# Cross-attention's keys and values made in the modulation stage and kept in DRAM

## The reference

```
x = x + memory_cross_attention(rms_norm(x, norm_xattn[l]), rms_norm(mem, norm_mem[l]), wq[l], wkv[l], wo[l])

q = (xn @ wq)                    # 4 heads of 128
kv = (memn @ wkv)                # keys and values, 4 heads each: 1024 columns
p = softmax(q k^T / sqrt(128))
o = (p v) @ wo
```

## Time and profile before

| | us |
|---|---|
| median of 3 runs | 3963.09 (3961.88 to 3965.83) |
| the profiled execution | 3962.45 |
| its span | 3961.1 |
| TensorE busy | 3767.7 (95%) |
| VectorE busy | 2579.8 (65%) |
| ScalarE busy | 1794.8 (45%) |
| POOL busy | 1484.2 (37%) |

### The profile page before, as it was taken

The page is one execution under the profiler, slowest core; times in us unless marked ns, Lnnn a source line. Parts: engine busy times, 40 slices in busy tenths (PEclk is TensorE's granted clock), DMA queues, the critical chain, the costliest instruction groups (busy, mean ns, idle before and its releaser), DMA issues.

```text
span 3961.1 us, 64430 instructions
## 1 busy us (share of the span) xinstructions
PE 3767.7 (95%) x27348; PEld 3208.4 (81%) x27348; DVE 2579.8 (65%) x3660; ACT 1794.8 (45%) x2792; POOL 1484.2 (37%) x726
## 2 busy tenths in 40 slices
PE   6898999999999999989999999999889999999998
PEld 3787888787877887888788888888778878888887
DVE  0436644785378897669879667876657775445457
ACT  1446443654355444445444444444545553333334
POOL 0332443133323440004354444444644434444443
PEclk8999999999999999999999999999899999999999
DMA  9653765355534552015366465657345435554553
GB/s 389 250 233 133 285 242 208 147 208 194 218 149 170 183 186 91 23 73 185 140 198 233 183 237 195 225 223 275 147 159 204 171 128 192 190 191 174 191 190 128
DMA packets 60848, 746.92 MB, mean 189 GB/s; under 512 B 7040, under 2 KB 9216, under 8 KB 17168
## 3 DMA queue, kind: packets, MB, share of 16 engines
q1 hardware_dynamic: 49536, 696.74, 46.5%
q0 software_dynamic: 8960, 43.95, 2.9%
q10 hardware_dynamic: 2064, 2.10, 0.2%
HBM read 725.92 MB, written 16.84 MB: 188 GB/s over the span
## 4 chain that ended last, share of the span: by engine, by line
PE 80%; DVE 12%; ACT 5%; DMA 2%; issue 1%; POOL 0%; another core or an unknown queue 0%; SPq 0%; DVEq 0%; ACTq 0%; POOLq 0%
PE ps L380 45%; PE ps L381 23%; DVE pieces L333 2%; PE ps L2283 2%; PE ps L811 2%; ACT pieces L317 2%; DMA ring<-in_ada 2%; PE ps L3652 1%; DVE opa L587 1%; DVE r L1224 1%; PE ps L1953 1%; DVE scr L608 1%; PE ps L660 1%; ACT scr L691 1%; DVE scr L392 0%
## 5 line engine op out<-in xcount | busy, mean ns | idle before, releaser
L380 PE MATMUL ps<-opa,pieces 128*128 128x512 f32 x6192 | 2241.5, 405 | 49.2 <-DVE pieces L333 32.7
L351 POOL TENSOR_TENSOR pieces<-ring,pieces 128x1024 fp32r<-128x1024 f32 x539 | 1344.8, 2495 | 2142.3 <-ACT pieces L317 2125.0
L381 PE MATMUL ps<-opa,pieces 128*128 128x256 f32 x6192 | 1739.0, 281 | 0.0
L317 ACT ACTIVATE pieces<-ring 128x1024 fp32r<-128x1024 f32 (+1 forms) x1110 | 1098.5, 1036 | 815.0 <-PE ps L381 812.8
L380 PEld LDWEIGHTS ps<-opa,pieces 128*128 128x128 f32 x6192 | 1168.6, 189 | 345.8 <-issue 33.9
L381 PEld LDWEIGHTS ps<-opa,pieces 128*128 128x128 f32 x6192 | 1174.8, 190 | 7.5 <-issue 5.0
L333 DVE TENSOR_TENSOR pieces<-ring,pieces 128x1024 fp32r<-128x1024 f32 (+1 forms) x571 | 715.4, 1253 | 257.9 <-ACT pieces L317 254.9
L380 PE MATMUL ps<-opb,pieces 128*128 128x512 f32 x2304 | 817.6, 396 | 14.1 <-DVE pieces L333 14.1
L381 PE MATMUL ps<-opb,pieces 128*128 128x256 f32 x2304 | 652.6, 283 | 0.0
L380 PEld LDWEIGHTS ps<-opb,pieces 128*128 128x128 f32 x2304 | 434.2, 188 | 123.6 <-issue 20.1
L381 PEld LDWEIGHTS ps<-opb,pieces 128*128 128x128 f32 x2304 | 434.7, 189 | 0.1
(11 more groups left out here) (450 smaller groups left out, 3568.3 us busy)
## 6 DMA issues: line engine op xcount, KB each, us to landing
ring<-in_up SPq DMA_DIRECT2D x64, 2048.0 KB, 7.7
ring<-in_down SPq DMA_DIRECT2D x64, 2048.0 KB, 7.7
ring<-in_win SPq DMA_DIRECT2D x56, 2048.0 KB, 7.8
ring<-in_ada SPq DMA_DIRECT2D x48, 2048.0 KB, 12.1
ring<-in_wout SPq DMA_DIRECT2D x24, 2048.0 KB, 8.3
ring<-in_evin SPq DMA_DIRECT2D x18, 2048.0 KB, 8.0
ring<-in_evout SPq DMA_DIRECT2D x8, 2048.0 KB, 8.1
ring<-in_xkv SPq DMA_DIRECT2D x8, 2048.0 KB, 7.8
```

The costliest lines, as they stand in the source:

```text
L317: a.do.activation(K.parts_of(p)[0][:, s, :], w[:, s, :], ACT.Copy).then_inc(*K.hi.up((p, h)))
L351: g.do.tensor_tensor(lo[:, s, :], w[:, s, :], hi[:, s, :].bitcast(F), ALU.subtract).then_inc(*K.lo2.up(p))
L380: pe.do.matmul(r3(b[:, 0:512], 2), hi[:, k, :], both(op, k), start=i == 0, stop=False)
L381: t = pe.do.matmul(b[:, 0:256], lo[:, k, :], half(op, 0, k), start=False, stop=i == kt - 1)
```

## The change

- `plan` puts the eight key/value slabs of both layers (four each, 16 tiles) at the front, in the order: key/value slab, two modulation slabs, next key/value slab. They are gone from the layers.
- The front becomes `pe_memory`, `act_memory`, `dve_memory` and `pool_memory`: tile, modulation slab, tile, modulation slab (the last two slabs after tile 14). The memory is loaded first, into the half of `x1` that will later hold the tokens, and is scaled and split into `opa` for layer 0 and `opb` for layer 1. The memory's sum of squares is taken once, in tiles 0 and 1. The context's follows in tiles 6 to 9, and `pe_norm` with its helpers goes.
- Context, tokens, constants and pooling weights load later: the context ahead of slab 3 on SyncE's queue, the rest on POOL's queue from gate tile 2 on.
- Keys and values of a layer are normalized into `xa`, the values turned, and POOL stores them to a DRAM tensor `xmem`. `pool_mem` loads 1 MB of it back ahead of cross-attention, in place of the memory.
- In `pe_xattn` the head steps (`pe_xheads`) are a side generator of the query tiles, one step after every three blocks: during tile n the values of head n-2 and scores and turnings of head n-1. Head 3 comes after the last query tile. The heads' result goes to a buffer of its own, `xop`.
- S5's column steps move from the key/value tiles to the output projection of layer 0 (its tiles 4 and on), where the memory's squares were. Two loads for S5 wait until after the last output tile of cross-attention.

```
 def plan(self):
...
-        for c in range(16):
-            raw(("ada", 0, c), ada[c])
+        for l in range(2):
+            gemm(("xkv", l), [D["xkv"][l * 4 + i] for i in range(4)])
+        tiles, todo = todo, []
+        for i in range(0, 16, 2):
+            todo.append(tiles[i])
+            for c in (i, i + 1):
+                raw(("ada", 0, c), ada[c])
+            todo.append(tiles[i + 1])
...
 def sp_weights(K):
+        if i == 3:
+            sp.do.dma_start(K.X[:, :, 256:512], r3(K.D["xin"], 16)[:, :, 256:512]).then_inc(*K.load["xctx"].up("xctx", 16))
...
 def sp_start(K):
     K.sp.do.dma_start(K.cols, K.D["cols"]).then_inc(*K.load["cols"].up("cols", 16))
+    K.sp.do.dma_start(K.X[:, :, 0:256], r3(K.D["mem"], 16)).then_inc(*K.load["mem"].up("mem", 16))
...
+def pe_memory(K):
+    pe = K.pe
+    for t in range(16):
+        l, n = divmod(t, 8)
+        side = pe_beside_memory(K, t)
+        pe_tile(K, t, K.opb if l else K.opa, ("nmem", l, "h"), (K.dve, ("xkv", l, n)), side, 5)
+        drain(side)
+        if t == 0:
+            pe.wait_ge(*K.dve.of(("silu", 1)))
+        for c in beside_memory(t):
+            pe_ada(K, 0, c, K.xb)
+            pe_turning(K)
+            K.turning = (0, c)
...
+def act_memory(K):
+    a.wait_ge(*K.load["mem"].of("mem"))
+    for k in range(16):
+        act_scaled(K, K.opa, ("nmem", 0, "h"), k, memory_block(K, k), gain(0, k))
+    act_feed(K, 0)
+    for t in range(16):
+        act_feed(K, t + 1)
+        if t < 2:
+            for k in range(8 * t, 8 * t + 8):
+                act_square(K, ("nmem",), k, memory_block(K, k), 1)
+        if t == 2:
+            act_std(K, ("nmem",), 1e-5, K.rmem)
+        if 2 <= t < 6:
+            for k in range(4 * t - 8, 4 * t - 4):
+                act_scaled(K, K.opb, ("nmem", 1, "h"), k, memory_block(K, k), gain(1, k))
...
+def dve_memory(K):
+    for k in range(16):
+        dve_scaled(K, K.opa, ("nmem", 0, "h"), k, memory_block(K, k), gain(0, k))
+    dve_feed(K, 0)
+    for t in range(16):
+        dve_feed(K, t + 1)
+        if t < 2:
+            for k in range(8 * t, 8 * t + 8):
+                dve_square(K, ("nmem",), k, 1)
+        if t == 2:
+            dve_rstd(K, ("nmem",), K.rmem)
+            v.wait_ge(*K.dve.of(("nmem", "rstd")))
+            dve_memory_out(K, 0)
+            dve_memory_out(K, 1)
...
+        if t >= 2:
+            dve_memory_out(K, t)
...
 def pool_mem(K, l):
     g.wait_ge(*K.dve.of(("mx", l, 15)))
-    g.do.dma_start(K.mem, r3(K.D["mem"], 16)).then_inc(*K.load["mem"].up(("mem", l), 16))
+    g.wait_ge(*K.load["xk_out"].of(("xk", l)))
+    g.wait_ge(*K.load["xv_out"].of(("xv", l)))
+    g.do.dma_start(K.xa, K.D["xmem"][l]).then_inc(*K.load["kv"].up(("kv", l), 16))
...
 def pe_xattn(K, l):
+    for n in range(7):
+        side = pe_xheads(K, l, h, n) if n else pe_totals(K, ("nx", l))
+        if n < 4:
+            pe_tile(K, p + n, K.opb, ("nx", l, "h"), (K.dve, ("xq", l, n)), side, 3 if n else 6)
+        drain(side)
     p = K.first["xo", l]
     for n in range(16):
-        pe_tile(K, p + n, K.opb, ("xo", l), (K.dve, ("xx", l, n)))
+        pe_tile(K, p + n, K.xop, ("xo", l), (K.dve, ("xx", l, n)))
+
+def pe_xheads(K, l, h, i):
+    if 0 <= i - 2 < 4:
+        n = i - 2
+        pe_values(K, h, n, [[K.VX[:, j, n * P:(n + 1) * P] for j in range(2)]], (K.dve, ("xo", l, n)))
+        yield
+    if 0 <= i - 1 < 4:
+        n = i - 1
+        pe.wait_ge(*K.load["kv"].of(("kv", l)))
+        pe.wait_ge(*K.dve.of(("xqn", l, n)))
+        for qt in range(2):
...
+            pe.do.matmul(b[:, 0:256], K.QX[:, n, qt * P:qt * P + P], K.KX[:, n, :], start=True, stop=True).then_inc(*K.prod.up(h.key("sc", n, qt)))
+            yield
+        for qt in range(2):
+            pe_turn(K, h, n, qt)
+            yield
```

More of the change, by code:

```diff
@@ new lines, in pe_beside_memory @@
+def pe_beside_memory(K, t):
+    if t == 2:
+        yield
+        K.pe.wait_ge(*K.load["io"].of("io"))
+        pe_total(K, ("nmem",), 1)
+        yield
+    if t == 11:
+        pe_total(K, ("n1", 0, 1))
+        yield
+    if t == 15:
+        pe_turning(K)
+        yield
+    l, n = divmod(t - 1, 8)
+    if t and n > 3:
+        yield from pe_xvturn(K, l, n - 4)
+def act_memory(K):
+    a = K.a
+    gain = lambda l, k: K.col(f"norm_mem{l}", k)
+    a.wait_ge(*K.load["mem"].of("mem"))
[12 more added lines that the diff above has]
+                act_scaled(K, K.opb, ("nmem", 1, "h"), k, memory_block(K, k), gain(1, k))
+        if t == 6:
+            a.wait_ge(*K.load["xctx"].of("xctx"))
+        if 6 <= t < 10:
+            for k in range(4 * t - 24, 4 * t - 20):
+                act_square(K, ("n1", 0, 1), k, x_at(K, 1)(k))
+        if t == 11:
+            act_std(K, ("n1", 0, 1), 1e-6, K.rstd)
+        l, n = divmod(t - 1, 8)
+        if t and n > 3:
+            act_xvturn(K, l, n - 4)
+        for c in beside_memory(t):
+            act_row(K, 0, c)
@@ L1000, in pe_gates @@
     for n in range(16):
-        pe_tile(K, p + n, K.opa, hk, (K.dve, ("gsum", l, s, n)))
+        side = pe_xvturn(K, 1, 3) if (l, s) == (0, 1) and n == 0 else None
+        pe_tile(K, p + n, K.opa, hk, (K.dve, ("gsum", l, s, n)), side)
         pe_fill(K, p + n)
@@ L1580, in pool_block1 @@
     g = K.g
+    pool_memory(K)
     pool_start(K)
@@ L2873, in act_mixout @@
         act_part(K, K.opa, ("mx", l), k, mixed(K, l, k))
+    columns = iter(()) if l else act_s5_columns(K)
     for n in range(17):
@@ L2878, in act_mixout @@
             act_ahead(K, ("nx", l), n - 1, xb(K, n - 1), ("mixo", l, n - 1), nx(n - 1), K.opb)
-        if 6 <= n < 14:
-            a.wait_ge(*K.load["mem"].of(("mem", l)))
-            for k in (2 * n - 12, 2 * n - 11):
-                act_square(K, ("nmem", l), k, K.mem[:, k, :], 1)
+        if n >= 4:
+            next(columns, None)
 def dve_mixout(K, l):
@@ L2889, in dve_mixout @@
         dve_part(K, K.opa, ("mx", l), k, mixed(K, l, k))
+    columns = iter(()) if l else dve_s5_columns(K)
     for n in range(16):
@@ L2915, in pe_xattn @@
 def pe_xattn(K, l):
-    pe, p, h = K.pe, K.first["xq", l], heads3(K, l)
-    for n in range(4):
-        side = None if n else pe_totals(K, ("nx", l), ("nmem", l))
-        pe_tile(K, p + n, K.opb, ("nx", l, "h"), (K.dve, ("xq", l, n)), side, 6)
-    p = K.first["xkv", l]
-    for n in range(8):
-        if l == 0 and n == 6:
-            pe_s5_rows(K)
-        side = pe_xvturn(K, l, n - 5) if n > 4 else None
-        pe_tile(K, p + n, K.opa, ("nmem", l, "h"), (K.dve, ("xkv", l, n)), side, 5)
-        if n > 4:
-            drain(side)
@@ L2928, in pe_xattn @@
-    drain(pe_xvturn(K, l, 3))
-    pe.wait_ge(*K.act.of(("xv", l, 3)))
-    pe.wait_ge(*K.dve.of(("xkvn", l, 7)))
-    for i in range(6):
-        if i < 4:
-            for qt in range(2):
-                b, was = K.xb.take(K.act, h.key("ex", i, qt))
-                K.bank[h.key("sc", i, qt)] = b
-                pe.wait_ge(*was)
-                pe.do.matmul(b[:, 0:256], K.QX[:, i, qt * P:qt * P + P], K.KX[:, i, :], start=True, stop=True).then_inc(*K.prod.up(h.key("sc", i, qt)))
-        if 0 <= i - 1 < 4:
-            for qt in range(2):
-                pe_turn(K, h, i - 1, qt)
-        if 0 <= i - 2 < 4:
-            n = i - 2
-            pe_values(K, h, n, [[K.VX[:, j, n * P:(n + 1) * P] for j in range(2)]], (K.dve, ("xo", l, n)))
+    p, h = K.first["xq", l], heads3(K, l)
@@ L3051, in pool_xo @@
         pool_square(K, ("nf", l), k)
+    if l == 0:
+        K.g.wait_ge(*K.tile.of(K.first["up", 0, 0] - 1))
+        pool_s5_first(K)
 def pe_ffn(K, l):
```

203 lines of the change are left out of this document (95 added, 108 removed).

## The result

The changed kernel took 3936.62 us, median of 4 runs (3933.15 to 3938.3), the kernel before 3963.34 in the same job. The ratio is 0.9927, 95% interval 0.9914 to 0.9941: 29 us faster by the interval's middle (27 between the medians), and above the forecast range of 3897 to 3930. The profiled executions stand 24.2 us apart (3938.3 and 3962.45) where the sum gave 53.8, so 29.6 us are to be found. Followed tile by tile against the trace before, they are: the front 18.8 us (from the second on, the gate tiles came 72.3 us later, with 53.5 forecast), the output projection of layer 0's mixer 5.4, the two cross-attention stretches 4.4, and 1 us in small shifts.

The account below looks back on a forecast made before the run. The front was taken as DMA-bound with idle TensorE, cross-attention tiles as the reverse. Savings of 107.3 us less 52.0 for later gates and 1.5 for low clock gave 53.8 off, so 3909 us; range 3897 to 3930.

Parts of the forecast that it names:

- the sum: Whole kernel: 107.3 us saved, less 52.0 for later gates and 1.5 for low clock, gives 53.8 us gained.
- 54.3 and 53.0 us of savings: Cross-attention, layers 0 and 1: time saved from first query tile to first output tile by moving key/value tiles forward.
- TensorE sets the pace, narrowly. Last memory tile ends at 157.6.: Front: a pair of tiles with two slabs takes TensorE 16.1 us, three slabs on the DMA engines 14.7.
- three slabs of 4.9 us on the DMA engines are 14.7 us: Front: DMA time for three slabs, set against TensorE's 16.1 us per pair of tiles.
- Ring stalls ahead of tile 2: Front: second key slab waits for POOL's split and the context; tile 2 starts at 39.6 instead of 37, 2.6 us.
- Rival 1: Front: ring late for each key slab; 10 us, 3919 at chance 0.12, or slower, 3974, at 0.02.
- Rival 2: Front: VectorE becomes the bound if two operations per tile are stretched; 11 us, 3920, chance 0.08.
- The S5 columns beside the output projection, where they take the place of 16 squarings: Layer 0's output projection: the moved column steps were taken as hidden, at a cost of nothing.
- Query tiles with heads: Cross-attention: four query tiles with head products beside them and head 3's tail, 37.9 us in layer 0, 36.6 in layer 1.
- Heads beside the tiles: Cross-attention: head products woven into query tiles, 6.5 us there, in place of a heads stage of 15.8 and 15.4 us.
- The wrong condition given ahead: Front: forecast is wrong if memory tiles stand more than 8.5 us apart; 8.05 expected with their slab.
- The other condition: Cross-attention: forecast is wrong if query tiles with heads take over 12 us each.

Follow-up runs that it names:

- experiment 13: Changed kernel with only the reordered front of experiment 12, its modulation slabs of half the bytes multiplied twice; memory tile 15 ended at 157.4 us.
- experiment 12: Changed kernel with front reordered, S5 columns behind the addition, heads behind the query tiles one step apart; 3915.9 us, ratio 0.9876 to the kernel before.
- experiment 4: Changed kernel with the front's 16 modulation slabs moved in half and the half multiplied twice; memory tile 15 ended at 177.9 us instead of 176.1.
- experiment 6: Changed kernel with the context one place later in SP's queue, behind the second key slab; memory tile 15 ended at 170.2 us instead of 176.1.
- experiment 7: Changed kernel with one S5 column step per output tile, behind the addition; first output tile's end to first query tile 82.4 us instead of 85.9.
- experiment 1: Changed kernel with ScalarE splitting both pieces of the next key slab together on odd memory tiles; tile 15 ended at 183.6 us instead of 176.1.
- experiment 10: Changed kernel with the first head's steps 5 operand blocks apart instead of 3 in the second query tile; that tile 8.5 us, stretches 38.3 and 38.0.
- experiment 11: Changed kernel with heads behind the query tiles, one step apart; first query tile to first output tile 36.5 and 37.4 us.
- experiment 8: Changed kernel with heads behind the query tiles, each by itself; first query tile to first output tile 51.3 and 49.4 us.

## Why the prediction was wrong

The direction and the trade were right, and 54.3 and 53.0 us of savings measured 52.7 and 50.2. The forecast failed on terms it had priced at a few us or at nothing.

- *"TensorE sets the pace, narrowly. Last memory tile ends at 157.6."* This is the step that failed. The start was exact (19.22 for 19.2), and TensorE's own work nearly so: experiment 13 ends at 157.4 with 2.4 us of waits in it, where the forecast had 3.6. The kernel ended at 176.1. Of the 18.7 us between the two, 11.1 go with the orders of ScalarE, VectorE and SP (to 165.0 in experiment 12) and 7.6 with the bytes (to 157.4). The two don't simply add up: with the change's orders the bytes were worth nothing (experiment 4). My cycle counted split, landing and split, and left out what else stands in the same queues between the two pieces of a slab: the slabs came 18.4 to 20.2 us apart instead of 16.1.
- *"three slabs of 4.9 us on the DMA engines are 14.7 us"*, the other half of that step. No row of this kernel gives 4.9 us. There has 389 GB/s at a share of 0.94, which is 5.4 us for 2 MB and 16.2 us for three, no less than TensorE's 16.1. In experiment 12 the front moved 363 to 406 GB/s at shares of 0.92 to 1.01, 5.2 to 5.8 us a slab.
- *Ring stalls ahead of tile 2*, 39.6 forecast, 41.7 measured. The context's place alone is worth 5.9 us to the end of the front (experiment 6); I had seen it and put the whole stall at 2.6. The latency of 2.3 us and the 5.9 us for the context in that sum are in no row either; the slab issued at 25.45, with the context ahead of it, landed 13.8 us later, where the sum has 13.1.
- *Rival 1* named the slot, with a landing of 12.1 us and TensorE work of 18.5. Landings were 8.9, under its threshold of 10.7, and the key slab was late all the same. It had taken the odd piece as split 5 us after its tile; in the chain above VectorE's split of piece 5 ended at 70.5, 10.8 us after tile 3 (59.7). *Rival 2* had stretched operations as a load on VectorE. Load was not the matter (VectorE is busy 22.2 of 36.8 us from 63 to 100 us) but place: the stretched operation stood ahead of the one that TensorE waited for. The Trainium skill (SBUF — State Buffer, "Who interferes with whom") has the two engines exclude each other, and the rows agree: 3.68 us for four blocks, 3.42 for one split, 2.05 for one multiplication.
- *"The S5 columns beside the output projection, where they take the place of 16 squarings"*, hidden at nothing: 5.4 us, of which experiment 7 gives back 3.5. Not the amount of work but its place ahead of the addition. Of the other 1.8 us, 1.6 stand in the second halves of the projection's first two tiles, ahead of the columns: 7.25 us for both against 5.63 in the kernel before, at a granted clock of 0.76 against 1.00, behind the same wait of 2.5 us. No experiment changes this place, and experiments 1, 4, 10 and 13 have 5.6 to 5.7 us at 1.00 there, the others 7.2 at 0.76. So it isn't the columns' cost; why the clock falls there in some runs stays open.
- *Query tiles with heads.* The products' time was right (the third and fourth tile take 8.25, 2.6 over a bare one), the tail exact (6.5 forecast, 6.46). Waits in the second tile were put at 1.9 us in layer 0 and 0.5 in layer 1 and came to 3.3 in both. I had charged a table load to layer 0 alone. Both layers load twice (for the deviation and the exponential), 1.28 us each; the drain that the Trainium skill gives (ScalarE: Activation LUTs, "What ACT_TABLE_LOAD costs") is again in no row: the square root above starts 0.01 us behind its load.
- *Heads beside the tiles* as a gain. The sum gave 37.9 with them and 38.8 without, and 36.5 without was measured. A head's products are TensorE's own work; only TensorE's idle time can be hidden, 3.3 of 13.0 us in experiment 11. Weaving left 2.6 us of that in the tail and brought 3.3 us of waits into the second query tile.

The wrong condition given ahead ("more than 8.5 us apart") was met at nine of the 15 intervals between memory tiles; two of the nine, behind tile 0 at the low clock and behind tile 14 with its two slabs, were in the sum. The other condition, query tiles over 12 us, wasn't met (10.8 at most).

## What to carry to other kernels

When a buffer is released by several in-order engines, its cycle is the sum of everything in their queues between the landing and the last release, not of the operations on that buffer: write the queues out. Some single cures in such a ring gain (-5.9 and -2.2 us), others only hand the wait to the next engine (+7.5; +2.7 and +0.7 are little or nothing in this spread), so judge them together. And weave small work beside tiles of the engine that bounds only for the idle time it hides, not for its length.

## What the runs showed of the hardware

A short wait of TensorE inside a tile can cost more than its length, and doesn't always. After 3.3 us of wait, the rest of tile 8 in experiment 1 ran at a granted clock of 0.58 (mostly the 1.2 GHz level), and the tile took 12.3 us instead of 6.1. After 4.4 us, tile 6 of the changed kernel took 11.9. But after 3.4 us in tile 2 of experiment 1 the clock stayed at the 2.4 GHz level. The heads in experiment 8 ran at 0.57 and took 27.9 us where 13.0 do at 1.00: of the 14.9 us, 9.0 are longer busy time and 5.8 more idle time. I had not expected either to be that large beside waits this short.
